# Windowed attention with query and key norms: who squares, how the last keys are normed, and in which order VectorE masks scores and copies keys

## The reference

```
def rms_norm_2(x, g):
    y = xf * lax.rsqrt(jnp.mean(xf * xf, axis=-1, keepdims=True) + EPS)
    return (y * g.astype(jnp.float32)).astype(x.dtype)

def mixer_a(h, w_qkv, q_gain, k_gain, w_o, cos, sin):
    qkv = (h @ w_qkv).reshape(B, S, A_GROUPS, 3, A_HEADS, HEAD_DIM)
    for g in range(A_GROUPS):
        q = partial_rope(rms_norm_2(qkv[:, :, g, 0], q_gain[g]), cos, sin)
        k = partial_rope(rms_norm_2(qkv[:, :, g, 1], k_gain[g]), cos, sin)
        v = qkv[:, :, g, 2]
        num, den, mx = dilated_group(q, k, v, dil, radius)
    ...
    wts = jnp.exp(mx - jnp.max(mx, axis=0, keepdims=True))
    num = jnp.sum(wts[..., None] * jnp.stack(nums, 0), axis=0)
    den = jnp.sum(wts * jnp.stack(dens, 0), axis=0)
    return (num / den[..., None]) ... @ w_o
```

## Time and profile before

| | |
|---|---|
| median of 3 runs | 3222.11 us (3220.30 to 3222.67) |
| profiled execution | 3229.45 us, its span 3227.7 us |
| TensorE, weight loads | 2908.2 us busy (90%), 2259.5 us (70%) |
| VectorE, ScalarE, GpSimd | 1185.6 us (37%), 907.4 us (28%), 784.1 us (24%) |
| attention, from its first projection to its last turned output | 1626.8 to 2239.8 us of the span |

### The profile page before, as it was taken

The page is one execution under the profiler, slowest core; times in us unless marked ns, Lnnn a source line. Parts: engine busy times, 40 slices in busy tenths (PEclk is TensorE's granted clock), DMA queues, the critical chain, the costliest instruction groups (busy, mean ns, idle before and its releaser), DMA issues. The chain is left out here.

```text
span 3227.7 us, 54770 instructions
## 1 busy us (share of the span) xinstructions
PE 2908.2 (90%) x24557; PEld 2259.5 (70%) x24557; DVE 1185.6 (37%) x1726; ACT 907.4 (28%) x1522; POOL 784.1 (24%) x218
## 2 busy tenths in 40 slices
PE   6987969989797697998999999998999989899998
PEld 4765858879685442333379988986788878678887
DVE  3334365646443600110355457563211123321111
ACT  3123132424213210100225443444322232232221
POOL 3320221302102000000122233221344434334442
PEclk8989979989898799999989999998999999899999
DMA  6211100110203199999722222212222322222231
GB/s 246 62 46 37 53 2 11 50 56 4 95 3 130 63 423 427 427 427 427 313 103 66 73 72 67 78 57 74 76 95 92 104 78 89 72 81 98 92 104 53
DMA packets 171629, 397.60 MB, mean 123 GB/s; under 512 B 9551, under 2 KB 99636, under 8 KB 146036
## 3 DMA queue, kind: packets, MB, share of 16 engines
q1 hardware_dynamic: 170416, 390.70, 32.9%
q10 hardware_dynamic: 980, 3.40, 0.3%
HBM read 387.71 MB, written 4.19 MB: 121 GB/s over the span
## 5 line engine op out<-in xcount | busy, mean ns | idle before, releaser
L179 POOL TENSOR_TENSOR weight_ring_lo<-weight_ring,weight_hi 128x2048 fp32r<-128x2048 f32 (+1 forms) x144 | 661.7, 4596 | 2009.7 <-ACT weight_hi L168 1970.3
L168 ACT CAST weight_hi<-weight_ring 128x2048 fp32r<-128x2048 f32 (+1 forms) x144 | 271.1, 1884 | 685.2 <-PE mlp_o L213 248.1
L213 PE MATMUL a_o<-weight_hi,latT_hi 128*128 128x512 f32 x576 | 178.9, 433 | 2.5 <-PEq L3159 2.5
L213 PE MATMUL a_o<-weight_ring_lo,latT_hi 128*128 128x512 f32 x576 | 159.6, 400 | 0.0
L213 PE MATMUL a_o<-weight_hi,latT_lo 128*128 128x512 f32 x576 | 157.7, 396 | 0.0
L213 PE MATMUL mlp_o<-weight_hi,mlp_hid_hi 128*128 128x512 f32 x512 | 139.2, 394 | 9.8 <-issue 9.8
L3035 DVE TENSOR_TENSOR x<-x,mlp_o 128x512 f32<-128x512 f32 x64 | 44.0, 687 | 282.2 <-PE mlp_o L213 282.2
L213 PEld LDWEIGHTS a_o<-weight_hi,latT_hi 128*128 128x128 f32 x576 | 133.7, 274 | 17.6 <-issue 8.7
L213 PEld LDWEIGHTS a_o<-weight_ring_lo,latT_hi 128*128 128x128 f32 x576 | 135.1, 270 | 9.0
L3020 DVE TENSOR_TENSOR mlp_hid<-mlp_hid,mlp_h 128x512 f32<-128x512 f32 x64 | 41.2, 685 | 271.8 <-ACT mlp_hid L2995 271.8
L213 PEld LDWEIGHTS a_o<-weight_hi,latT_lo 128*128 128x128 f32 x576 | 134.3, 270 | 8.1
(11 more groups left out here) (591 smaller groups left out, 5899.1 us busy)
## 6 DMA issues: line engine op xcount, KB each, us to landing
weight_ring<-in_mlp_w SPq DMA_DIRECT2D x64, 1024.0 KB, 5.1
weight_ring<-in_a_wqkv SPq DMA_DIRECT2D x36, 1024.0 KB, 5.1
weight_ring<-in_w_up SPq DMA_DIRECT2D x32, 1024.0 KB, 20.4
weight_ring<-in_w_gate SPq DMA_DIRECT2D x31, 1024.0 KB, 22.3
weight_ring<-in_w_down SPq DMA_DIRECT2D x31, 1024.0 KB, 20.8
weight_ring<-in_w_mod SPq DMA_DIRECT2D x24, 1024.0 KB, 5.7
weight_hi_spare<-in_w_up SPq DMA_DIRECT2D x12, 1024.0 KB, 20.2
weight_hi_spare<-in_w_gate SPq DMA_DIRECT2D x12, 1024.0 KB, 22.5
```

Of the source, the lines that this page charges most:

```text
L168: self.nc.scalar.copy(self.view(self.hi[:, q % 2], p, True), self.view(self.slots[self.slot[p]], p, True)).then_inc(self.hi_ready, 1)
L179: self.nc.gpsimd.tensor_tensor(self.view(self.lo[:, s], p, True), self.view(self.slots[s], p, True), self.view(self.hi[:, q % 2], p, True) ...
L213: last = nc.tensor.matmul(dst, left(a, HK * r + k), right(b, k), start=(r + a + b + k == 0), stop=(r == 1 and a == 1 and k == HK - 1))
```

## The change

It has four parts.

1. When ScalarE empties a bank of queries or keys, it first writes the squares of the bank (an `ACTIVATE` with the function Square, PSUM to SBUF) into the buffer that VectorE filled before, then copies the bank. `mean` no longer squares. The sum over 64 elements is split: three tiles one step earlier, the last tile at the old step, then the mean. The squares need no other table of functions: ScalarE's queue has 53 table loads in the whole program before and now.
2. Because ScalarE now writes into a buffer with other uses, it waits at the first bank of a part: at the keys for the rotation of the same round's queries (`normed` 4n+2), in round 3 for the move of the near sums, in rounds 4 and 5 for `out_ready`.
3. The last round's keys are scaled and rotated in two halves of four heads, the first at step 137 and the second at 138; TensorE waits for the first before it turns the first pair of heads and for the second before the third pair.
4. On VectorE, a step's `keep` and `maxima` stand ahead of its `write_k`.

```diff
--- before.py
+++ after.py
@@ -2415,2 +2415,3 @@
     tables_loaded = sem("a_tables_loaded")
+    sq_written = sem("a_squares_written")
     q_turned, k_turned = sem("a_q_turned"), sem("a_k_turned")
@@ -2507,2 +2508,4 @@
                     pe.wait_ge(normed, 4 * (n + 1))
+                elif hp == 2 and n + 1 == N_GROUP:
+                    pe.wait_ge(normed, 4 * (n + 1) + 2)
                 if tp_free:
@@ -2631,2 +2634,10 @@
                     act.wait_ge(st.used, p0 + m // NT + 1)
+                if part % 3 < 2:
+                    if j == 0 and part % 3:
+                        act.wait_ge(normed, 4 * n + 2)
+                    elif j == 0 and n == 3:
+                        act.wait_ge(num_moved, moved)
+                    elif j == 0 and n > 3:
+                        act.wait_ge(out_ready, 1)
+                    nc.scalar.activation(groups[n].sq[:, j], flat(acc[j][:]), ACT.Square).then_inc(sq_written, 1)
                 nc.scalar.copy((f.q, f.k, groups[n].v)[part % 3][:, j, :], flat(acc[j][:])).then_inc(emptied, 1)
@@ -2734,15 +2745,16 @@
 
-            def mean(i):
-                n = i // 2
-                x = (f.q, f.k)[i % 2]
-                sq = groups[n].sq
-                if i == 6:
-                    dve.wait_ge(num_moved, moved)
+            def sum_squares(i, j0, j1):
+                if i == 6 and j0 == 0:
                     dve.wait_ge(md_moved, moved)
-                dve.wait_ge(emptied, NT * (3 * n + i % 2 + 1))
-                step.link(dve, V.tensor_tensor(sq, x, x, ALU.mult))
-                step.link(dve, V.tensor_reduce(f.ms[:, i % 2], sq.rearrange("p j (h d) -> p j h d", d=HD), AX, ALU.add))
+                dve.wait_ge(sq_written, NT * i + j1)
+                sq = groups[i // 2].sq[:, j0:j1].rearrange("p j (h d) -> p j h d", d=HD)
+                step.mark(V.tensor_reduce(f.ms[:, i % 2, j0:j1], sq, AX, ALU.add))
+
+            def mean(i):
+                sum_squares(i, NT - 1, NT)
+                step.settle(dve)
+                dve.wait_ge(emptied, NT * (3 * (i // 2) + i % 2 + 1))
                 V.tensor_scalar(f.ms[:, i % 2], f.ms[:, i % 2], 1.0 / HD, EPS, ALU.mult, ALU.add).then_inc(meaned, 1)
 
-            def scale(i):
+            def scale(i, h=slice(0, GH)):
                 x = (f.q, f.k)[i % 2]
@@ -2751,17 +2763,25 @@
                     step.link(dve, V.tensor_scalar(f.gains[:, 0:3], f.gains[:, 0:3], HD ** -0.5, None, ALU.mult))
-                dve.wait_ge(rooted, i + 1)
-                step.link(dve, V.reciprocal(f.rt[:, i % 2], f.rt[:, i % 2]))
-                heads = x.rearrange("p j (h d) -> p j h d", d=HD)
-                step.link(dve, V.tensor_tensor(heads, heads, f.rt[:, i % 2].unsqueeze(3).to_broadcast([P, NT, GH, HD]), ALU.mult))
-                gain = f.gains[:, 3 * (i % 2) + i // 2 % 3].unsqueeze(1).to_broadcast([P, NT * GH, HD])
-                rows = x.rearrange("p j (h d) -> p (j h) d", d=HD)
-                step.link(dve, V.tensor_tensor(rows, rows, gain, ALU.mult))
+                if h.start == 0:
+                    dve.wait_ge(rooted, i + 1)
+                    step.link(dve, V.reciprocal(f.rt[:, i % 2], f.rt[:, i % 2]))
+                n_head = h.stop - h.start
+                heads = x.rearrange("p j (h d) -> p j h d", d=HD)[:, :, h]
+                step.link(dve, V.tensor_tensor(heads, heads, f.rt[:, i % 2, :, h].unsqueeze(3).to_broadcast([P, NT, n_head, HD]), ALU.mult))
+                gain = f.gains[:, 3 * (i % 2) + i // 2 % 3].unsqueeze(1)
+                if n_head == GH:
+                    rows = x.rearrange("p j (h d) -> p (j h) d", d=HD)
+                    step.link(dve, V.tensor_tensor(rows, rows, gain.to_broadcast([P, NT * GH, HD]), ALU.mult))
+                else:
+                    for j in range(NT):
+                        step.mark(V.tensor_tensor(heads[:, j], heads[:, j], gain.to_broadcast([P, n_head, HD]), ALU.mult))
+                    step.settle(dve)
 
-            def rotate(i):
+            def rotate(i, h=slice(0, GH)):
                 n = i // 2
                 sq = groups[n].sq
-                heads = (f.q, f.k)[i % 2].rearrange("p j (h d) -> p j h d", d=HD)
-                prod = [sq[:, c, 0:GH * NT * 8].rearrange("p (j h d) -> p j h d", j=NT, h=GH) for c in range(4)]
+                n_head = h.stop - h.start
+                heads = (f.q, f.k)[i % 2].rearrange("p j (h d) -> p j h d", d=HD)[:, :, h]
+                prod = [sq[:, c, 0:n_head * NT * 8].rearrange("p (j h d) -> p j h d", j=NT, h=n_head) for c in range(4)]
                 x1, x2 = heads[:, :, :, 0:8], heads[:, :, :, 8:16]
-                cos, sin = (groups[n].rope[:, c].unsqueeze(2).to_broadcast([P, NT, GH, 8]) for c in range(2))
+                cos, sin = (groups[n].rope[:, c].unsqueeze(2).to_broadcast([P, NT, n_head, 8]) for c in range(2))
                 for dst, part, tab in ((prod[0], x1, cos), (prod[1], x2, sin), (prod[2], x2, cos), (prod[3], x1, sin)):
@@ -2771,3 +2791,3 @@
                 V.tensor_tensor(x2, prod[2], prod[3], ALU.add).then_inc(normed, 1)
-                dve.wait_ge(normed, 2 * (i + 1))
+                dve.wait_ge(normed, 2 * (i + 1) + (2 if h.start else 0))
 
@@ -2852,6 +2872,2 @@
             for m in range(N_TIME):
-                for n in range(N_GROUP):
-                    t = m - (PER_GROUP * (n + 1) if n + 1 < N_GROUP else LAST_TURN)
-                    if 0 <= t < 4:
-                        write_k(n, t)
                 for u, (n, hp, i, s) in enumerate(units):
@@ -2865,6 +2881,20 @@
                         maxima(u, 1)
+                for n in range(N_GROUP):
+                    t = m - (PER_GROUP * (n + 1) if n + 1 < N_GROUP else LAST_TURN)
+                    if 0 <= t < 4:
+                        write_k(n, t)
                 for i in range(2 * N_GROUP):
+                    if m == norm_slots(i)[0] - 1:
+                        sum_squares(i, 0, NT - 1)
                     for slot, do in zip(norm_slots(i), (mean, scale, rotate)):
-                        if m == slot:
+                        if m != slot:
+                            continue
+                        if i + 1 < 2 * N_GROUP or do is mean:
                             do(i)
+                        elif do is scale:
+                            scale(i, slice(0, GH // 2))
+                            rotate(i, slice(0, GH // 2))
+                        else:
+                            scale(i, slice(GH // 2, GH))
+                            rotate(i, slice(GH // 2, GH))
                 if m == FIRST_WEIGHTS:
```

More of the change, by code:

```diff
@@ L2733, in keep @@
                 V.tensor_copy(by_pair(groups[n].num[:, :, 2 * hp:2 * hp + 2, :]), pv[:]).then_inc(kept, 1)
-            def mean(i):
-                n = i // 2
-                x = (f.q, f.k)[i % 2]
-                sq = groups[n].sq
-                if i == 6:
-                    dve.wait_ge(num_moved, moved)
-                    dve.wait_ge(md_moved, moved)
-                dve.wait_ge(emptied, NT * (3 * n + i % 2 + 1))
-                step.link(dve, V.tensor_tensor(sq, x, x, ALU.mult))
-                step.link(dve, V.tensor_reduce(f.ms[:, i % 2], sq.rearrange("p j (h d) -> p j h d", d=HD), AX, ALU.add))
+            def sum_squares(i, j0, j1):
+                if i == 6 and j0 == 0:
+                    dve.wait_ge(md_moved, moved)
+                dve.wait_ge(sq_written, NT * i + j1)
+                sq = groups[i // 2].sq[:, j0:j1].rearrange("p j (h d) -> p j h d", d=HD)
+                step.mark(V.tensor_reduce(f.ms[:, i % 2, j0:j1], sq, AX, ALU.add))
+            def mean(i):
+                sum_squares(i, NT - 1, NT)
+                step.settle(dve)
+                dve.wait_ge(emptied, NT * (3 * (i // 2) + i % 2 + 1))
                 V.tensor_scalar(f.ms[:, i % 2], f.ms[:, i % 2], 1.0 / HD, EPS, ALU.mult, ALU.add).then_inc(meaned, 1)
-            def scale(i):
+            def scale(i, h=slice(0, GH)):
                 x = (f.q, f.k)[i % 2]
```

## The result

The changed kernel took 3208.28 us (median of 11 runs), the kernel before 3222.67 beside it. The ratio is 0.9951, with an interval of 0.9939 to 0.9963, so it is 15.8 us faster (11.9 to 19.7); the two medians themselves are 14.4 apart. I had said 3210, from 3203 to 3219.

A forecast was written before the change was run, and what follows sets the result against it. TensorE bounds the projection rounds, so only ending its waits counts. Terms -3.7 + 1.25 - 5.1 - 5.2 + 0 = -12.75 us take the median 3222.1 to 3209.4, said as 3210, range 3203 to 3219.

The forecast's parts named there:

- a): Norms: with squares off VectorE, five short TensorE waits behind the mean go, -3.7 us.
- The mean comes before that start: Norms: the mean runs before GpSimd's panel starts and costs some 0.2 us instead of 2.13.
- b): Second unit of strided rounds: squares on ScalarE add 0.5 to each of three waits, masks win 0.25 back; +1.25 us.
- c): Step 99: masks ahead of the key copy remove the wait of 1.77 and the half clock behind it, -5.1 us.
- d): Last round: masks no longer stand behind the third key copy, second unit's exponentials start earlier; -5.2 us.
- e): Fourth output tile: VectorE's product still waits for GpSimd's panel, so TensorE's wait of 4.75 stays; 0 us.
- The halves: Last norm in two halves: adds some 1.5 us to VectorE, hidden before TensorE asks for them.
- Rival 1: Fourth output tile: the product gets in ahead of GpSimd, 5.7 us more won, 3204 us; chance 0.12.
- Rivals 2 and 4: ScalarE late: 2, in strided rounds with half clock, 3219, chance 0.14; 4, pacing all unit rounds, 3238, chance 0.06.
- Rival 3: Step 99 keeps its half clock or the last round gives only its first wait; up to 3215, chance 0.10.

The follow-up runs named there:

- squares only: The changed kernel with key copies ahead of the masks again and the last keys normed in one piece; ratio 0.9989 to the kernel before, 6.6 us in the stage.
- masks first only: The kernel before with only masks and kept outputs moved ahead of the key copy, squares still on VectorE; ratio 0.996, 12.2 us in the stage.
- the low part ahead: The changed kernel with the output tiles' low part ahead of that step's mean, scaling, rotation and product on VectorE; ratio 0.9972, 9.8 us in the stage.
- one panel in eight: The changed kernel with one GpSimd panel, the one that blocked the mean, written as 8 instructions; ratio 0.996 to the kernel before, 12.8 us in the stage.
- squares twice: The changed kernel with each of ScalarE's 48 squares computed twice; ratio 0.9963 to the kernel before, 11.6 us in the stage.
- three split with the rounding moved: The changed kernel with the last three attention panels in 8 instructions each and ScalarE's last rounding two steps later; 3201.4 us, ratio 0.9931.

## Why the prediction was right, point by point

The sum was -12.75 and the stage gave 15.8. That 3210 lies within 2 us of 3208.28 is in part luck: the terms were 3.05 short, but the medians differ by less than the stage and the ratio say.

- **a)** Said -3.7, measured -4.8. All five waits went, and each gave some 0.2 more than its row. For a part of it the rows show why: the four transposes behind a wait take 0.66, and 0.60 without one. The rest is open. "The mean comes before that start" held in eleven norms and failed in the last one, by 0.2 us; that is e.
- **b)** Said +1.25, measured about 0. This term was mis-sized. The square costs what I said (0.49, 0.50 and 0.48 in squares only). But I let the masks' new place win 0.25 back at one of three waits, and it wins about 0.5 at each: ScalarE begins the first unit's exponentials that much sooner.
- **c)** Said -5.1, measured -5.0. The wait (said 1.75, measured 2.0) needed the masks' new place, as worked out. The half clock (said 3.4, measured 3.0) goes with the wait, as masks first only shows. But the wait is not enough for it: squares only keeps the wait and loses the half clock. Whether that comes from the missing wait of 1.28 or from the moment, the runs don't tell. Each part alone wins these 3.0 us, and both together win them once.
- **d)** Said -5.2, measured -5.9 (5.4 with masks first only). The second unit's exponentials start 4.04 us behind the first's (2176.77 and 2180.81), as said. The copy of 2205.35 now starts at 2186.17. It moved by 5.3 us more than the first exponentials, as worked out. By 2192 the round has won 3.0, nearly all of it the first wait, and by 2212 another 2.6. The waits for the two copies did not shrink together (3.77 and 2.46 before, 2.65 and 3.68 now); what is won there beside the first of them is half clock, 13.7 us of it from 2191 to 2216 before and 6.8 now.
- **e)** Said 0, measured 0, by the right mechanism and the wrong instruction. I had the product blocked; it was the mean, and the product behind it. By the rule of the Trainium skill ("SBUF — State Buffer", section "SBUF: two separate sides") GpSimd and a VectorE instruction with two SBUF inputs, or in a mode that uses both ports, shut each other out for a whole instruction, whichever begins first. The trace agrees in both directions: the mean took 4.42 behind GpSimd, and with the low part ahead GpSimd's panel took 6.65, which began 0.09 behind VectorE's product of 2.29. The mean has one SBUF input, so only the second case can cover it; in which mode it ran no view here shows.
- The halves cost nothing, as said, and bring nothing. VectorE needs 1.4 us more for them (8.25 in all against 6.84 in one piece). TensorE asks for the first half 10.4 us after the fourth output tile (2154.45 and 2164.80), not three steps of 2.8.

Rival 1 (the product gets in ahead of GpSimd) did not come. Its price leaves out what follows: one panel in eight and the low part ahead of the norm both take this wait away, and in both the norm behind it meets the next panel, so the 5.7 us would not have stayed. Rivals 2 and 4 (ScalarE late) fall with squares twice: even 48 squares more cost only 4.2 us, with no half clock in the strided rounds behind a wait of 1.71. Rival 3 fell with c and d. The errors of the terms do not cancel: a gave 1.1 more, b 1.35, d 0.7, and c 0.1 less, which is the 3.05 by which the sum was short.

## What to carry to other kernels

Where VectorE and GpSimd shut each other out, split the long instruction of the one that nobody waits for: eight of 128x256 took GpSimd 5.76 and 9.44 us instead of some 4.6, and the wait of 4.36 us fell to 0.54. Do it for all that follow as well, and look at what the saved time brings together next: in the stage, one panel split lost 3 us, and three split with the rounding moved won 4.7. And test parts alone: here each of two parts won the same 3.0 us of half clock.

## What the hardware showed that I had not expected

- What stands still beside GpSimd and what does not is seen side by side in the last round of the changed kernel (VectorE, while GpSimd ran from 2186.35 for 4.51 us):

```profile
2187.57 0.69 DVE L2736 TENSOR_TENSOR a_s<-a_sc,a_stride 128x512 f32<-128x512 f32 x1 [1.95 <-PE a_tp L2552]
2188.29 0.69 DVE L2738 TENSOR_REDUCE a_max_den<-a_s 128x4 f32<-128x512 f32 x1
2188.90 2.00 DVE L2841 TENSOR_TENSOR a_wt<-a_top,a_max_den 128x16 f32<-128x16 f32 x1
2190.93 0.17 DVE L2842 TENSOR_TENSOR a_wd<-a_wt,a_top 128x16 f32<-128x16 f32 x1
```

  A mask with scores from PSUM and a maximum run at their usual 0.69. The 128x16 with two inputs in SBUF waits for GpSimd's end at 2190.86. The next such one takes 0.17.
- A 128x32 and a 128x128 instruction of VectorE took 4.42 and 4.49 us though they need 0.18 and 0.29, because GpSimd had started 0.2 to 0.3 us before. It need not have two inputs in SBUF: the mean has one.
- Behind one and the same wait of 1.76 us TensorE's clock was at half (1.2 GHz) for 6.9 us, for 3.4 (granted 0.66 over 5.0 us), or not at all.
- The stage repeated to 0.2 us in two executions of the kernel before, while whole runs of one kernel differ by 10 and more.
